# The decay branch of the gated linear attention layers: a full-width split product against a plain fp32 product on four column bands

## The reference

```python
GLA_GATE_RANK = 16
...
q, k, v, g, a = _split(h @ w_in, [GLA_KEY_DIM, GLA_KEY_DIM, GLA_VAL_DIM, GLA_VAL_DIM, GLA_GATE_RANK])
logf = jax.nn.log_sigmoid((a @ w_a2 + b_a).astype(jnp.float32)) / GLA_GATE_TAU
...
o = rmsnorm(o, g_on).astype(h.dtype).reshape(B, L, GLA_VAL_DIM)
return (o * jax.nn.silu(g)) @ w_out, s
```

## Time and profile before

| | |
|---|---|
| runs of the kernel before | 1145.84, 1148.64, 1149.34 us; median 1148.64 |
| the profiled execution's own time | 1147.31 us |
| its span in the profile | 1145.6 us |
| PE busy | 1109.4 us, 97% of the span |
| DVE, ACT, POOL busy | 58%, 42%, 33% |
| DMA | 169.31 MB, mean 148 GB/s |
| instructions in the trace | 25429 |

### The profile page before, as it was taken

The page is one execution under the profiler, slowest core; times in us unless marked ns, Lnnn a source line. Parts: engine busy times, 40 slices in busy tenths (PEclk is TensorE's granted clock), DMA queues, the critical chain, the costliest instruction groups (busy, mean ns, idle before and its releaser), DMA issues. The chain is left out here.

```text
span 1145.6 us, 25429 instructions
## 1 busy us (share of the span) xinstructions
PE 1109.4 (97%) x10509; PEld 962.0 (84%) x10509; DVE 667.7 (58%) x1214; ACT 485.5 (42%) x955; POOL 382.0 (33%) x321
## 2 busy tenths in 40 slices
PE   8999999899999999989998999999999999999996
PEld 6889888899758988879955599999999889888875
DVE  6462255754999779767454555596445272245633
ACT  6542376643443322222363454322453352367542
POOL 5545213244313413114300044353345245311240
PEclk9999999999999999999999999999999999999998
DMA  5234233333314787884779932233220324334122
GB/s 174 98 111 166 93 111 114 127 83 100 111 58 147 239 274 233 288 298 155 258 300 409 374 112 89 64 107 120 91 75 3 111 87 160 105 106 153 56 74 78
DMA packets 125722, 169.31 MB, mean 148 GB/s; under 512 B 20441, under 2 KB 89689, under 8 KB 125600
## 3 DMA queue, kind: packets, MB, share of 16 engines
q1 hardware_dynamic: 113401, 152.85, 39.9%
q10 hardware_dynamic: 12206, 14.85, 3.6%
HBM read 151.22 MB, written 16.81 MB: 147 GB/s over the span
## 5 line engine op out<-in xcount | busy, mean ns | idle before, releaser
L756 POOL TENSOR_TENSOR w_lo<-raw,w_hi 128x512 fp32r<-128x512 f32 (+2 forms) x267 | 359.5, 1377 | 688.0 <-ACT w_hi L1547 688.0
L792 PE MATMUL psum<-h_hi,w_hi 128*128 128x272 f32 (+1 forms) x1488 | 433.9, 292 | 4.3 <-DVE h_lo L2528 2.3
L794 PE MATMUL psum<-h_hi,w_lo 128*128 128x272 f32 (+1 forms) x1488 | 430.2, 289 | 0.0
L793 PE MATMUL psum<-h_lo,w_hi 128*128 128x272 f32 (+1 forms) x1488 | 428.0, 288 | 0.0
L792 PEld LDWEIGHTS psum<-h_hi,w_hi 128*128 128x128 f32 (+1 forms) x1488 | 279.2, 188 | 17.5 <-issue 14.2
L793 PEld LDWEIGHTS psum<-h_lo,w_hi 128*128 128x128 f32 (+1 forms) x1488 | 279.5, 188 | 0.1
L794 PEld LDWEIGHTS psum<-h_hi,w_lo 128*128 128x128 f32 (+1 forms) x1488 | 278.9, 187 | 0.0
L1547 ACT ACTIVATE w_hi<-raw 128x1024 fp32r<-128x1024 f32 (+1 forms) x137 | 135.5, 1034 | 117.7 <-PE psum L794 82.1
L792 PE MATMUL psum<-w_hi,h_hi 128*128 128x512 f32 (+2 forms) x416 | 150.5, 362 | 1.0 <-DVE dsa_score_s L2625 0.8
L794 PE MATMUL psum<-w_hi,h_lo 128*128 128x512 f32 (+2 forms) x416 | 146.2, 351 | 3.0 <-issue 3.0
L793 PE MATMUL psum<-w_lo,h_hi 128*128 128x512 f32 (+2 forms) x416 | 146.1, 351 | 0.7 <-issue 0.7
(11 more groups left out here) (334 smaller groups left out, 1387.3 us busy)
## 6 DMA issues: line engine op xcount, KB each, us to landing
smp_keys<-in_cache_k_dram SPq DMA_DIRECT2D x128, 256.0 KB, 4.6
raw<-in_gla_w_in_dram SPq DMA_DIRECT2D x23, 1024.0 KB, 5.3
raw<-in_dsa_w_in_dram SPq DMA_DIRECT2D x17, 1024.0 KB, 5.3
spare<-in_cache_v_dram SPq DMA_DIRECT2D x34, 512.0 KB, 8.0
raw<-in_cache_v_dram SPq DMA_DIRECT2D x30, 512.0 KB, 7.8
gla_s_in<-in_state_gla_dram SPq DMA_DIRECT2D x16, 512.0 KB, 7.5
raw<-in_gla_w_out_dram SPq DMA_DIRECT2D x8, 1024.0 KB, 6.5
out_dram<-gla_s_in ACTq DMA_DIRECT2D x16, 512.0 KB, 3.7
```

The costliest lines, as they stand in the source:

```text
L756: pool.tensor_tensor(copies(key, pair_view(w_lo, key)[:, k]), raw_copies(key, k), copies(key, pair_view(w_hi, key)[:, k].bitcast(F32)), AL ...
L792: pe.matmul(out, lh, rh, start=start, stop=False)
L793: pe.matmul(out, lh, rl, start=False, stop=False)
L794: return pe.matmul(out, ll, rh, start=False, stop=stop)
```

## The change

1. `a` is no longer one of the split weights. Its weight goes by a DMA of its own into `w_a` (128 x 8 x 16, fp32) and DVE multiplies it by the gain ahead of the norm.
2. The first product, `low_rank`: plain fp32 from `XT`, 32 matmuls with 16 stationary columns. Token tile j is put on column band j (the last one with the 32 sample tokens, 160 columns). It claims bank 5.
3. The second product, `gate_rank`: called ahead of token tile 1 of value half 1 (so behind its tile 0). 16 matmuls of 16 x 128, one token tile for each row band and bank (0 to 3), and four for the sample tokens in bank 5.
4. Value half 1 claims its banks from the tuple (1, 6, 7, 4, 0) in place of all eight.
5. DVE scales `a` in four pieces, then reads z from psum itself: five additions of the bias into `qg`. ACT waits for all five, then takes |z| of the whole 128 x 2176 from SBUF, exp and log. DVE's last step takes min and difference in one instruction.
6. `w_a2` is loaded whole onto each row band; `QSLOT` is 1 and `fin` lies over other memory.

```diff
-                f_item((L, "a"), w, 2 * GH * GDK + 2 * D, RANK)
+                c0 = 2 * GH * GDK + 2 * D
+                items.append(((L, "a"), w[:, c0:c0 + RANK].rearrange("(k p) n -> p k n", p=P), KT, RANK, "a"))
...
-                f_job((L, "a"), [((L, "a"), 0, P)], "a", range(NBANK), None, None if L else decode_rows)
-
-                pe.wait_ge(*on("a", (L, "a"), 1))
-                pe.wait_ge(*on("gla_small", L))
-                bs = claim(next_bank(), ("z", L, "s"), ("z_read", L, "s"))
-                for h in range(GH):
-                    r = slice(h * NS, h * NS + RANK)
-                    b = claim(next_bank(), ("z", L, h), ("z_read", L, h))
-                    pe.matmul(psum[:, b, 0:SEQ], w_a2[r, h * GDK:(h + 1) * GDK], a_t[r, 0:SEQ],
-                              start=True, stop=True).then_inc(*sig("z", L, h))
...
-                t_job([(L, "v", 1, kh) for kh in range(2)], (L, "v", 1), BLK, "v", range(NBANK))
+                def low_rank():
+
+                    pe.wait_ge(*on("w_a", L))
+                    b = claim(5, ("proj", (L, "a")), ("a", L, 3))
+                    for k in range(KT):
+                        for j in range(4):
+                            n = TOK - j * P if j == 3 else P
+                            mm = pe.matmul(psum[j * NS:j * NS + RANK, b, 0:n], w_a[:, k, :],
+                                           XT[:, k, j * P:j * P + n], start=k == 0, stop=k == KT - 1)
+                    mm.then_inc(*sig("proj", (L, "a"), also=((("item", (L, "a")),),)))
+
+                def gate_rank(x, t):
+
+                    if (x, t) != (0, 1):
+                        return
+                    pe.wait_ge(*on("a", L, 3))
+                    pe.wait_ge(*on("gla_small", L))
+                    for t in range(TILES):
+                        claim(5 if t == SMP else t, ("z", L, t), ("z_read", L, t))
+                    for h in range(GH):
+                        for t in range(NP_T):
+                            r = slice(t * NS, t * NS + RANK)
+                            mm = pe.matmul(psum[:, t, h * P:(h + 1) * P], w_a2[r, h * GDK:(h + 1) * GDK], a_t[r, 0:P],
+                                           start=True, stop=True)
+                            if h == GH - 1:
+                                mm.then_inc(*sig("z", L, t))
...
+                low_rank()
+                t_job([(L, "v", 1, kh) for kh in range(2)], (L, "v", 1), BLK, "v", (1, 6, 7, 4, 0), gate_rank)
...
-                for h in range(GH):
-                    act.wait_ge(*on("z", L, h))
-                    act.activation(soft[:, h, 0:SEQ], psum[:, bank_of("z", L, h), :], ACT.Abs,
-                                   bias=b_a[:, h:h + 1]).then_inc(*sig("z_abs", L, h))
...
-                after_item(L, "a")
-                act.wait_ge(*on("z_abs", L, "s"))
+                act.wait_ge(*on("z_read", L, SMP))
+                act.activation(soft[:], qg[:], ACT.Abs).then_inc(*sig("z_abs", L))
+                act.wait_ge(*on("z_abs", L))
...
-                f_scaled((L, "a"), a_t[:], "a")
+                dve.wait_ge(*on("proj", (L, "a")))
+                for j in range(4):
+                    r = slice(j * NS, j * NS + RANK)
+                    n = TOK - j * P if j == 3 else P
+                    dve.tensor_tensor(a_t[r, 0:n], psum[r, bank_of("proj", (L, "a")), 0:n],
+                                      rstd[r, j * P:j * P + n], ALU.mult).then_inc(*sig("a", L, j))
...
+                for t in range(TILES):
+                    n = rows(t)
+                    dve.wait_ge(*on("z", L, t))
+                    dve.tensor_tensor(qg[:, :, cols(t)],
+                                      psum[:, bank_of("z", L, t), 0:GH * n].rearrange("p (h t) -> p h t", h=GH),
+                                      b_a[:].unsqueeze(2).broadcast_to([P, GH, n]), ALU.add).then_inc(*sig("z_read", L, t))
+                dve.wait_ge(*on("z_read", L, SMP))
                 dve.wait_ge(*on("z_soft", L))
-                link(dve.tensor_tensor(qg[:], qg[:], soft[:], ALU.subtract))
+                link(dve.scalar_tensor_tensor(out=qg[:], in0=qg[:], scalar=0.0, in1=soft[:], op0=ALU.min,
+                                              op1=ALU.subtract))
```

More of the change, by code:

```diff
@@ L204, in program @@
         sq_end = place["at"]
+        fin = at("fin", [P, 6, TILES], F32, sq_at)
         sq_junk = at("sq_junk", [P, D], BF16, sq_at + size([P, TOK], F32))
         h_s = at("h_s", [P, KT, NS], F32, sq_at + size([P, TOK], F32))
+        w_a = sb("w_a", [P, KT, RANK])
         arena, arena_end = place["at"], nc.sbuf_usable_end
@@ L402, in program @@
         for n, it in enumerate(items):
+            if it[4] == "a":
+                continue
             key, choice = it[0], list(range(RAW))
@@ L503, in small @@
                     sp.dma_start(w_a2[0:RANK, :], gla_w_a2[j]).then_inc(*sig("gla_small", L, 0, n=16))
-                    for h in range(1, GH):
-                        sp.dma_start(w_a2[h * NS:h * NS + RANK, h * GDK:(h + 1) * GDK],
-                                     gla_w_a2[j, :, h * GDK:(h + 1) * GDK]).then_inc(*sig("gla_small", L, 2, n=16))
+                    for x in range(1, 4):
+                        sp.dma_start(w_a2[x * NS:x * NS + RANK, :], gla_w_a2[j]).then_inc(*sig("gla_small", L, 2, n=16))
                     sp.dma_start(b_a[:], gla_b_a[j].rearrange("(h p) -> p h", p=P),
@@ L554, in _ @@
                 L = key[0]
+                if kind == "a":
+                    if L:
+                        sp.wait_ge(*on("proj", ("item", (0, "a"))))
+                    sp.dma_start(w_a[:], src).then_inc(*sig("raw_a", L, n=16))
+                    continue
                 if kind == "K" and key[2] in (0, 10, 12):
@@ L755, in _ @@
                     pool.wait_ge(*on("split_hi", key, x * 2 // len(pieces(key)) if n else ("k", x)))
-                    pool.tensor_tensor(copies(key, pair_view(w_lo, key)[:, k]), raw_copies(key, k),
-                                       copies(key, pair_view(w_hi, key)[:, k].bitcast(F32)), ALU.subtract)\
+                    pool.tensor_tensor(pair_view(w_lo, key)[:, k], raw_view(key)[:, k],
+                                       pair_view(w_hi, key)[:, k].bitcast(F32), ALU.subtract)\
                         .then_inc(*sig("split", key, x, also=((key,),) if k.stop == items[index[key]][2] else ()))
@@ new lines, in gate_rank @@
+                def gate_rank(x, t):
[12 more added lines that the diff above has]
+                                mm.then_inc(*sig("z", L, t))
+                    r = slice(3 * NS, 3 * NS + RANK)
+                    for h in range(GH):
+                        mm = pe.matmul(psum[:, 5, h * NS:(h + 1) * NS], w_a2[r, h * GDK:(h + 1) * GDK],
+                                       a_t[r, P:P + NS], start=True, stop=True)
+                    mm.then_inc(*sig("z", L, SMP))
@@ L1565, in split_hi @@
                     k = slice(half * kk // 2, (half + 1) * kk // 2) if len(pieces(key)) > 1 else slice(0, kk)
-                    copy(copies(key, pair_view(w_hi, key)[:, k]), raw_copies(key, k)).then_inc(*sig("split_hi", key, half))
+                    copy(pair_view(w_hi, key)[:, k], raw_view(key)[:, k]).then_inc(*sig("split_hi", key, half))
             def first_split(pieces_now):
@@ L2329, in gla @@
                     decode_input(L)
+                dve.wait_ge(*on("raw_a", L))
+                dve.tensor_tensor(w_a[:], w_a[:], gains[:, L, :].unsqueeze(2).broadcast_to([P, KT, RANK]), ALU.mult)\
+                    .then_inc(*sig("w_a", L))
                 dve.wait_ge(*on("gla_small", L))
@@ L2341, in gla @@
                         link(dve.tensor_copy(head_row[h * NS:(h + 1) * NS, :], seq_row[:]))
[L2342 to L2345, removed]
-                dve.wait_ge(*on("z_abs", L, "s"))
-                for h in range(GH):
-                    dve.tensor_scalar(qg[:, h, SEQ:TOK], psum[:, bank_of("z", L, "s"), h * NS:(h + 1) * NS],
-                                      b_a[:, h:h + 1], 0.0, ALU.add, ALU.min).then_inc(*sig("z_read", L, "s"))
-                dve.wait_ge(*on("z_read", L, "s"))
+                for t in range(TILES):
[5 more added lines that the diff above has]
+                dve.wait_ge(*on("z_read", L, SMP))
                 dve.wait_ge(*on("z_soft", L))
-                link(dve.tensor_tensor(qg[:], qg[:], soft[:], ALU.subtract))
+                link(dve.scalar_tensor_tensor(out=qg[:], in0=qg[:], scalar=0.0, in1=soft[:], op0=ALU.min,
+                                              op1=ALU.subtract))
                 for h in range(GH):
```

20 lines of the change are left out of this document (1 added, 19 removed).

## The result

The changed kernel takes 1168.6 us (median of four, 1165.96 to 1171.27) against 1148.11 us for the kernel before (median of four, the three of the table above and one more); ratio 1.0181, 95% interval 1.0164 to 1.0197. It is slower by 20.5 us, and the interval lies clear of 1. The profiled execution took 1165.96 us, 18.65 more than the profiled one of before.

The account below looks back on a forecast made before the run. PE, busy 97% of the span, was taken as the bound, with a chain without slack beside it. Later keys 8.8 + 4.8 and clock 3.0 on 1147.3 gave 1163.9, plus 1.3 for the median: 1165 us, range 1157 to 1171.

Parts of the forecast that it names:

- The wait for the bank: First keys wait for ACT's copies of value half 1: 12 us (layer 0), 8 (layer 3); start 8.8, 4.8 later.
- The first product: In layers 0 and 3, 32 fp32 matmuls on four column bands take 2.3 us, bounds 2.1 and 7.8.
- The rival of bands in turn: First product's bands do not overlap: it takes 7.8 us, chain 5.5 us later per layer, 1176 us; chance 0.05.
- The second product: In layers 0 and 3, 16 matmuls on four row bands take 2.1 us, bounds 1.1 to 2.8.
- DVE's small copies: Layer 0, ahead of reading z: four of eight held by POOL some 1.25 us each, costing 2.6 us.
- The running sums beside POOL: POOL's earlier split of the first key weights holds DVE up as often as before; nothing in the sum.
- The clock: After each wait ahead of the keys PE runs at 1.2 GHz: 1.5 us lost per wait, 3.0 in all.
- the rival without loss of clock: The waits ahead of the keys come but PE's clock stays: 1162 us; chance 0.14.
- At nothing: Zero cost: DVE's product of `w_a` and gain, new DMAs, one weight item less, bank counter in layers 1 and 2.
- The sum: Whole kernel: 8.8 + 4.8 + 3.0 = 16.6 us on 1147.3, giving 1163.9 for the profiled execution.
- The rival on the other side: At the first key matmul, copies are in time: the saved 6.8 us come through, 1142 us; chance 0.03.

Follow-up runs that it names:

- Experiment 3: Kernel before the change with only its bank counter moved, by seven ahead of the keys and one behind: 1165.24 us, ratio 1.0144.
- experiment 1: Changed kernel with keys, queries and key transposes on another bank order (2, 3, 5, 6, 7, 4, 0, 1): 1148.46 us, ratio 1.0003.
- experiment 2: Changed kernel with its own banks, but ACT copies value half 1 ahead of its wait for DVE's running sums: 1144.59 us, ratio 0.9969.
- Experiment 6: Changed kernel with the two loops of the first product swapped, so one column band works after another: 1172.66 us, ratio 1.0218.
- experiment 7: Changed kernel with new key banks, early ACT copies, late small DVE copies, and the counter of layers 1 and 2 restored: 1141.22 us, ratio 0.9950.
- experiment 5: Changed kernel with DVE's eight small copies of layer 0 moved behind its reading of z: 1163.66 us, ratio 1.0144.
- Experiment 4: Changed kernel with unused filler matmuls (92 in layer 0, 68 in layer 3) ahead of the first key product: 1161.82 us, ratio 1.0126.
- 8: As experiment 7, but with ACT's copies of value half 1 left where the change has them: 1143.98 us, ratio 0.9977.
- experiment 9: As experiment 7, but with the second product ahead of tile 0 of value half 1: 1146.09 us, ratio 0.9984.
- 10: Kernel before the change with only ACT's copies of value half 1 moved ahead of its wait for the running sums: 1147.27 us, ratio 1.0005.

## Why the prediction was right, step by step

- **The wait for the bank**, the step on which everything rests, was right in place, releaser and length: 12.6 and 8.3 us measured, 12 and 8 forecast; the keys of layer 0 at 83.05 (83.5 forecast), those of layer 3 later by 4.1 (4.8 forecast). Experiment 3 makes the wait without the new branch; 1 and 2 take it away in two ways.
- **The first product**: 2.3 us as forecast, from the sample products' rate. Experiment 6 shows the overlap that the rate assumed. The rival of bands in turn was set too high at 7.8; they take 6.3.
- **The second product** was sized too large: 1.02 us, not 2.1, just below its lower bound of 1.1. The row that I went by, with 256 moving columns at 89 ns a record, was the wrong neighbour, and I read it wrongly: its weights are 32 x 128, not the same as here. The z products of before in the earlier trace rows have these weights, 16 x 128 on four row bands, and 512 moving columns: eight records in 0.97 us, 121 ns each. A quarter of the columns would be 30 ns, and 32 were measured, so with these weights the time went with the moving columns. The 1.1 us less shortened the chain of layer 3, more than the 0.7 by which that term came out short. It also makes the saving on PE larger than the 3.4 us per layer that I took: experiment 7 has 4.3.
- **DVE's small copies**: right, four of them held. Reading z starts 2.9 us later than in experiment 5 (50.75 against 47.90; forecast 2.6), and the keys follow with 2.9. Without these rows the forecast for layer 0 would have been 80.9.
- **The running sums beside POOL**: running sums, `mid` and the four subtractions took 11.63 us in layer 0 against 11.61 before, so the total is as forecast, though other instructions are held: the running sums are longer (8.96 against 5.89 us), `mid` and the subtractions shorter.
- **The clock**: the mechanism was right, the size was not: 2.0 and 2.6 us measured, 1.5 and 1.5 taken, within the bounds. Experiment 4 gives 4.5 back. So idleness does bring the low clock back, as the Trainium skill has it (TensorE: Matmul & The Clock Gate, Part 1), and the rival without loss of clock falls.
- **At nothing**: the bank counter did belong there. Four places on, it makes PE wait 1.2 us for DVE at the first reused bank of layer 0's output (L2317) and 1.1 us for ACT in layer 1, and it takes away 1.4 us for `idx_k_old` and 0.8 for `dsa_score_s`. By the sample products of layer 1 at 358.51 us, before 347.94, PE is 10.6 us late, only 0.3 more than at the gates of layer 0. Experiments 1 and 2 have the same four waits as the change, and 7, 8 and 9, whose counter is moved on again, those of before.
- What that list should not have left at nothing is the rest of layers 1 and 2, 1.6 of the 1.9 us, with a new wait of 2.2 us for `smp_keys` (in that part of layer 1 before has one of 3.0 us without a releaser). From the gates of layer 0 to the end of value half 0 of layer 3 each of the nine profiled kernels with the new branch took longer than the kernel before, by 1.3 us (experiment 7) to 8.2 (experiment 1); the two with the old branch (experiments 3 and 10) came within 0.6. With the counter of before it is still 1.3 to 3.6. The cause is open. One candidate that no run tests is the order in which weights and cache pages take the slots of `raw`, since `a` takes none any more and `QSLOT` is 1 in place of 2. If it is this, it is the change's own cost, and the new branch would be worth more without it.
- **The sum** came out as 1163.9 for the profiled execution, measured 1165.96. The terms were off by -0.5 and -0.7 (keys), +1.6 (clock) and +1.9 (layers 1 and 2), with 0.3 less elsewhere, so errors of both signs met. The median is 2.6 above the profiled execution and not 1.3 as before, which gives the rest to 1168.6; it was forecast as 1165 and lies inside the range. The rival on the other side, with 1142, is what the same branch gives once the banks, ACT's order and the place of DVE's small copies are changed: experiment 7, 1141.2.

## What to carry to other kernels

When a step is added to or taken from a list that takes buffers in turn, write down for the first instructions behind it which buffer they now claim and who frees it: here value half 1 got a tuple of its own and the counter twelve turns fewer per layer, which is four places on among eight banks. That made a wait for something long done into one for the last items of another engine's list, 20 us with hardly a change in any busy time. If such a wait appears, move the turn or the late reader before judging the edit itself: the same branch measured 1168.6 us as it came, 1144.6 with ACT's copies of value half 1 placed earlier, and 1141.2 with the banks of the keys, those copies and DVE's small copies all changed.

## What the runs showed of the hardware

- A short rest can be enough to lose PE's clock, but not each time. After a wait of 2.50 us (experiment 1, layer 0) and one of 1.46 us among small matmuls (experiment 9, layer 0), PE ran at 1.2 GHz and lost some 1.3 and 2.6 us, in the second case more than the wait. After 1.53 us among the same small matmuls (experiment 9, layer 3) and 1.63 us (experiment 2, layer 0) it ran at 2.4 GHz at once. After the 12.6 and 8.3 us of the changed kernel it lost 2.0 and 2.6, no more than that.
- Products on row bands: 32 records of 16 x 128 weights and 128 moving columns took 1.02 us on four bands, 32 ns each. The eight sample ones, with 32 moving columns and all on one band, took 0.9 us, 0.11 us each.
- A DVE copy of 32 x 32 or 32 x 8 elements takes 0.16 to 0.17 us alone and 1.2 us beside POOL's subtractions, in all four cases of the changed kernel.
